# Softmax sums carried by DMA and mixed work spread over the attention steps in an eight-core encoder layer

## The reference, cut to what matters

```
a = rms_norm(h, g_mix);  z = a @ w_in            # 2048 -> q 1024, k 1024, v 1024, u 1024, gv 1024
q, k = partial_rope(q), partial_rope(k)          # first 16 of 64 dims
s_c  = softmax(q_c k_c^T / 8), c = 0, 1          # 8 heads, two components of 64 dims, 2048 keys
o    = rms_norm(s_0 v - lam * s_1 v) * 0.8       # per head, 128 wide
g    = gelu(u) * (w_spatial . layer_norm(gelu(gv)) + b)   # 128x128 position mixing in each chunk
h   += [o, g] @ w_out
h   += (silu(conv3(G)) * conv3(U)) @ w_down      # [G, U] = rms_norm(h) @ w_up, 2 x 5632
h   += (p @ w_ple_up) * sigmoid(rms_norm(h) @ w_ple_gate)
y    = rms_norm(h, g_final)
```

## Time and profile before

| | |
|---|---|
| time, median of 3 runs | 2069.48 us (2062.49 to 2089.54) |
| the profiled execution's own time | 2064.24 us |
| its span (slowest core, 7) | 2062.7 us |
| spans of the 8 cores | 2053.6 to 2062.7 us |
| granted TensorE clock, mean of each core | 0.983 to 0.987 of full speed |
| busy: TensorE, DVE, ACT, POOL | 1917.6, 999.0, 749.4, 186.3 us |

### The profile page before, as it was taken

The page is one execution under the profiler, slowest core; times in us unless marked ns, Lnnn a source line. Parts: engine busy times, 40 slices in busy tenths (PEclk is TensorE's granted clock), DMA queues, the critical chain, the costliest instruction groups (busy, mean ns, idle before and its releaser), DMA issues.

```text
span 2062.7 us, 31107 instructions; the slowest of 8 cores (2053.6 to 2062.7 us)
## 1 busy us (share of the span) xinstructions
PE 1917.6 (93%) x11708; PEld 1059.0 (51%) x11708; DVE 999.0 (48%) x1305; ACT 749.4 (36%) x1039; POOL 186.3 (9%) x281
## 2 busy tenths in 40 slices
PE   5988999987889999988999999999999999999994
PEld 1433455554445555545666654566654566644441
DVE  3645201254444544554566641366641366643667
ACT  4621111104887777765222210122210022233553
POOL 5600000000000000001000000000000010001000
PEclk9998999999999999999999999999999999999997
DMA  9750344366002333328644444444444464444603
GB/s 223 221 109 14 69 82 62 53 120 195 1 1 42 52 54 60 52 52 134 111 73 75 78 75 75 78 79 75 74 75 78 82 103 77 71 72 83 108 26 138
DMA packets 60371, 170.43 MB, mean 83 GB/s; under 512 B 10816, under 2 KB 15168, under 8 KB 60096
## 3 DMA queue, kind: packets, MB, share of 16 engines
q0 software_dynamic: 34992, 125.58, 36.3%
q1 hardware_dynamic: 25232, 42.86, 6.6%
HBM read 279.29 MB, written 8.39 MB: 139 GB/s over the span
## 4 chain that ended last, share of the span: by engine, by line
PE 81%; DVE 6%; ACT 5%; issue 4%; DMA 3%; SPq 1%; POOL 1%; DVEq 0%; ACTq 0%; POOLq 0%
PE ps L336 81%; ACT big L339 4%; DVE big L342 3%; DMA big<-xo 1%; SPq L559 1%; DVE big L354 1%; DVE big L345 1%; DMA big<-wup 1%; POOL big L349 1%; DVE big L351 1%; DMA big<-xa 0%; DVEq L170 0%; DMA big<-big 0%; DMA big<-posa 0%; DVE big L349 0%
## 5 line engine op out<-in xcount | busy, mean ns | idle before, releaser
L336 PE MATMUL ps<-big 128*128 128x342 bf16 (+3 forms) x11708 | 1917.6, 330 | 125.1 <-ACT big L339 51.0
L336 PEld LDWEIGHTS ps<-big 128*128 128x128 bf16 (+1 forms) x11708 | 1059.0, 98 | 982.1 <-issue 257.9
L339 ACT ACTIVATE big<-big 128x1024 f32<-128x1024 f32 (+8 forms) x547 | 423.4, 792 | 925.8 <-DVE big L342 703.0
L342 DVE TENSOR_TENSOR big<-big 128x342 f32<-128x342 f32 (+8 forms) x424 | 306.1, 735 | 224.0 <-ACT big L339 190.2
L339 ACT ACTIVATE big<-ps 128x684 bf16<-128x684 f32 (+1 forms) x432 | 294.6, 705 | 178.2 <-PE ps L336 173.0
L345 DVE SCALAR_TENSOR_TENSOR big<-big 128x1024 f32<-128x1024 f32 (+1 forms) x228 | 258.5, 1134 | 207.2 <-ACT big L339 197.6
L342 DVE TENSOR_TENSOR big<-ps,big 128x1026 f32<-128x1026 f32 (+4 forms) x239 | 210.7, 897 | 284.1 <-PE ps L336 271.0
L342 DVE TENSOR_TENSOR big<-big,ps 128x342 f32<-128x342 f32 (+1 forms) x96 | 83.1, 866 | 202.6 <-PE ps L336 201.4
L402 POOL DMA_DIRECT2D big<-wup x88 | 46.5, 528 | 539.4 <-PE ps L336 508.7
L339 ACT ACTIVATE big<-ps,big 128x512 bf16<-128x512 f32 x50 | 34.0, 686 | 159.4 <-PE ps L336 159.4
L402 POOL DMA_DIRECT2D big<-wo x48 | 25.5, 532 | 518.5 <-PE ps L336 508.9
(11 more groups left out here) (25 smaller groups left out, 64.5 us busy)
## 6 DMA issues: line engine op xcount, KB each, us to landing
big<-wup POOLq DMA_DIRECT2D x88, 512.0 KB, 5.7
big<-wo POOLq DMA_DIRECT2D x48, 512.0 KB, 5.1
big<-xa SPq DMA_DIRECT2D x32, 512.0 KB, 7.2
big<-wdn POOLq DMA_DIRECT2D x32, 480.0 KB, 5.3
big<-xo SPq DMA_DIRECT2D x16, 512.0 KB, 9.9
big<-wg POOLq DMA_DIRECT2D x16, 512.0 KB, 13.7
y<-big SPq DMA_DIRECT2D x32, 256.0 KB, 2.2
big<-wdn POOLq DMA_DIRECT2D x16, 448.0 KB, 4.9
```

Of the source, the lines that this page charges most:

```text
L336: P.op("pe", lambda e: e.matmul(out, lhsT=lhsT, rhs=rhs, start=start, stop=stop), reads=reads, writes=writes, inc=inc)
L339: P.op("act", lambda e: e.activation(out=out, in_=in_, func=func, **kw), reads=reads, writes=writes)
L342: P.op(en, lambda e: e.tensor_tensor(out=out, in0=a, in1=b, op=op), reads=reads, writes=writes)
```

## The change

- The first V half uses banks 6, 7, 0, 1, 2, 3 in turn. `halo_norm` is called between the two pairs of tables, not ahead of both.
- `spatial()` is taken out of the q stage. `spatial_mm` (bank 7 only) is called in steps 3, 8 and 12 of the units 0 to 5, the halo part after it.
- The loads of h move from the stage's end into steps 6 of the units 1 to 15, and to the attention's end.
- The sums are copied to `SM`, SP writes the 4 rows that differ to DRAM (into y, which is overwritten at the end), and two further DMAs read them back, spread over all 128 partitions, into `LA` and `LB`. DVE adds the two, ACT takes one `Ln` and one `Exp` of 684 columns. `sum3(selw[c])` and its `split3` are gone; `post_b` moves to step 1 of the unit after.
- The fill matmuls are spread over the steps 2 to 15 by `FILL`, two or three in each.
- At unit 23 seven more weight slots are opened where K lay. `hg`, `xp` and the FFN's buffers change places for that.
- At the attention's end the leftover fill and 15 of 16 matmuls of block 2's first tiles are issued ahead of the last unit's `post_b`; the copies for the FFN come out of `late`.
- At the final norm `Ln` is called once on a dummy, and the last squares go into the sum by a second matmul. Four multiplications of block 0 move behind it.

```diff
         def halo_norm():
-            rstd_bcast(ACC[0][:, 0:2], R_ACC[0], 2, rown[:, 1024:1026], R_rown[2], 4)
-            rstd_tok(ACC[0][:, 0:128], R_ACC[0], 1, 16, R_rtok[4], 5)
+            rstd_bcast(ACC[1][:, 0:2], R_ACC[1], 2, rown[:, 1024:1026], R_rown[2], 4)
+            rstd_tok(ACC[1][:, 0:128], R_ACC[1], 1, 16, R_rtok[4], 5)
         def pre_steps():
-            load_halo(0, 0)
+            load_halo(1, 0)
             yield
-            load_halo(0, 1)
+            load_halo(1, 1)
             yield
-            yield
+            P.inherit(R_tco, R_XS)
+            P.inherit(R_ang, R_XS + R_SQ + [R_ACC[0]])
+            yield from table_steps(0, 1024, TO, roth, R_roth, R_tco)
             halo_norm()
             yield
-            P.inherit(R_tco, R_XS)
-            P.inherit(R_ang, R_XS + R_SQ + R_ACC)
-            yield from table_steps(0, 1024, TO, roth, R_roth, R_tco)
             yield from table_steps(1, NT, (TC, TS), rown, R_rown, R_tca[0])
         steps = pre_steps()
@@ -749,7 +746,7 @@
         for hf_ in range(2):
             for t in range(8):
                 P.inherit(R_V[8 + t][hf_], [R_lam])
-        tok_proj(vitems, v_epi(0), [6, 7], hook)
+        tok_proj(vitems, v_epi(0), [6, 7, 0, 1, 2, 3], hook)
 ...
-        def spatial():
-            if sp_i[0] >= 16:
-                return
+        def spatial_mm():
             grp, hh = sp_i[0] // 8, sp_i[0] % 8
-            b = (6, 7)[sp_i[0] % 2]
-            sx, R_sx = SPT[sp_i[0] % 2], R_SPT[sp_i[0] % 2]
+            b = 7
+            sx, R_sx = SPT[sp_i[0] % 2], R_ut[sp_i[0] % 2]
 ...
-        SPT = [V(ZRO, F32, 512), V(ZRO + 2048, F32, 512)]
-        R_SPT = [Reg(), Reg()]
+        SPT = [ut[0][:, 0:512], ut[1][:, 0:512]]
 ...
-            else:
-                for _ in range(3):
-                    spatial()
-        while sp_i[0] < 16:
-            spatial()
 ...
+        def h_first(i, gate):
+            P.dma("sp", lambda e: e.dma_start(out=h[:, 2 * i:2 * i + 2, 0:512], in_=src_h[0][i]), DS_h[i], after=gate + oldh)
+            P.dma("sp", lambda e: e.dma_start(out=h[:, 2 * i:2 * i + 2, 512:684], in_=src_h[1][i][:, :, 0:172]), DS_h[i], after=oldh)
+            for j in (2 * i, 2 * i + 1):
+                for b in range(2):
+                    R_h[j][b].w = (DS_h[i].sem, DS_h[i].cnt)
+        def h_last(i, gate, after=()):
+            P.dma("sp", lambda e: e.dma_start(out=h[:, 2 * i:2 * i + 2, 684:1024], in_=src_h[1][i][:, :, 172:512]), DS_h[i],
+                  reads=[R_h[2 * i][0]], after=gate + list(after) + oldh)
+            for j in (2 * i, 2 * i + 1):
+                R_h[j][2].w = (DS_h[i].sem, DS_h[i].cnt)
+        def h_tail(after):
+            for i in range(2):
+                src = xh_d[i].rearrange("p (a b) -> p a b", a=8)[:, :, 0:2]
+                P.dma("sp", lambda e: e.dma_start(out=h[:, 8 * i:8 * i + 8, 1024:1026], in_=src), DS_hh, after=list(after) + oldh)
+            for j in range(16):
+                R_h[j][2].r = {0: (DS_hh.sem, DS_hh.cnt)}
+        SM = h[:, 0, 684:1026]
+        LB = [h[:, 1, 684:1026], h[:, 2, 684:1026]]
 ...
             if kt == 15:
                 cpy(XO, ps[:, 4:6, 0:NB], [Rb[4], Rb[5]], [R_XO])
-                split3(ps[:, 6, 0:NB], [Rb[6]])
+                cpy(SM, ps[:, 6, 0:NB], [Rb[6]], [R_sm])
+                yb = y_d[0, 4 * (k // 16 % 2):4 * (k // 16 % 2) + 4, 0:NB]
+                P.dma("sp", lambda e: e.dma_start(out=yb, in_=h[0:128:32, 0, 684:1026]), DS_yb, reads=[R_sm], writes=[R_yb])
+                P.dma("sp", lambda e: e.dma_start(out=LA, in_=yb[0:2, :].partition_broadcast(128)), DS_l, reads=[R_yb], writes=[R_la])
+                P.dma("sp", lambda e: e.dma_start(out=h[:, 1:3, 684:1026], in_=yb[2:4, :].partition_broadcast(128)), DS_l, reads=[R_yb],
+                      writes=[R_lb])
+                R_la.w = R_lb.w = (DS_l.sem, DS_l.cnt)
 ...
-        def post_a(u, c):
-            R, Rr = ((R0, R_r0), (R1, R_r1))[c]
-            sum3(selw[c])
-            act(R, ps[:, 7, 0:NB], AF.Ln, [Rb[7]], [Rr])
-            act(R, R, AF.Exp, [], [Rr], scale=-1.0)
-            if c == 0:
-                tt(OO, XO[:, 0, :], R, ALU.mult, [R_XO, Rr], [R_oo])
-            else:
-                stt(R, XO[:, 1, :], neglam, R, ALU.mult, ALU.mult, [R_XO, R_lam], [Rr])
-                tt(OO, OO, R, ALU.add, [Rr], [R_oo])
-                tt(RM, OO, OO, ALU.mult, [R_oo], [R_rm])
-                split3(RM, [R_rm])
+        def post_add(u):
+            for c in range(2):
+                tt(LA[:, c, :], LA[:, c, :], LB[c], ALU.add, [R_lb], [R_la])
+        def post_ln(u):
+            act(LA, LA, AF.Ln, [], [R_la])
+        def post_exp(u):
+            act(LA, LA, AF.Exp, [], [R_la], scale=-1.0)
+        def post_o(u):
+            tt(OO, XO[:, 0, :], LA[:, 0, :], ALU.mult, [R_XO, R_la], [R_oo])
+            stt(LA[:, 1, :], XO[:, 1, :], neglam, LA[:, 1, :], ALU.mult, ALU.mult, [R_XO, R_lam], [R_la])
+            tt(OO, OO, LA[:, 1, :], ALU.add, [R_la], [R_oo])
+            tt(RM, OO, OO, ALU.mult, [R_oo], [R_rm])
+            split3(RM, [R_rm])
         def post_b(u):
             sum3(onesb)
-            tsc(R0, ps[:, 7, 0:NB], 1.0 / 128, EPS, ALU.mult, ALU.add, [Rb[7]], [R_r0])
-        def post_c(u):
+            tsc(RM, ps[:, 7, 0:NB], 1.0 / 128, EPS, ALU.mult, ALU.add, [Rb[7]], [R_rm])
+        def post_rs(u, i):
+            if i == 0:
+                act(RM, RM, AF.Ln, [], [R_rm])
+            else:
+                act(RM, RM, AF.Exp, [], [R_rm], scale=-0.5)
+        def post_out(u):
             b, hh = units[u]
-            lnexp(R0, R_r0)
-            stt(mixA[:, hh, b * NB:(b + 1) * NB], OO, gsubc, R0, ALU.mult, ALU.mult, [R_oo, R_r0, R_lam], [R_qb[hh][b]])
+            stt(mixA[:, hh, b * NB:(b + 1) * NB], OO, gsubc, RM, ALU.mult, ALU.mult, [R_oo, R_rm, R_lam], [R_qb[hh][b]])
 ...
+        sp_done = [False]
+        wonce = []
         gen = itertools.chain(wout_gen(0, [7]), wout_gen(1, [7]))
+        FILL = [0, 0, 3, 2, 2, 2, 2, 2, 3, 2, 2, 2, 2, 3, 3, 2]
         nstep = 16 * 24
         for k in range(nstep + LAG):
+            u, st = k // 16, k % 16
+            if u == 23 and st == 0:
+                for i in range(7):
+                    sl = Slot(Z3 + i * 4096, True)
+                    P.inherit(sl.reg, R_kT[0][i] + R_kT[1][i])
+                    wfree.append(sl)
+                    wonce.append(sl.reg)
+                pump()
             if k < nstep:
                 emit_qk(k)
-            u, st = k // 16, k % 16
-            fl = 9 <= u < 24 and st in (1, 2, 3, 4, 9, 10, 11, 12)
-            if fl:
-                fill(gen, 2)
+            nf = FILL[st] if 9 <= u < 24 else 0
+            fill(gen, nf - nf // 2)
+            if u < 9 and st in (3, 8, 12):
+                if sp_i[0] < 16:
+                    spatial_mm()
+                elif not sp_done[0]:
+                    spatial_halo()
+                    sp_done[0] = True
+                    for r in R_hacc:
+                        P.inherit(r, R_ut)
             ka = k - LAG
+            if u >= 2 and st == 1:
+                post_b(u - 2)
             if ka >= 0 and ka % 16 != 0:
                 if ka % 16 == 1:
                     emit_av(ka - 1)
                 emit_av(ka)
-            if fl:
-                fill(gen, 2)
+            fill(gen, nf // 2)
+            if u >= 24:
+                continue
             if u < 23 and st == 9:
                 q_pad(u + 1)
-            if st in (7, 15):
-                flush_sq()
-            if u < 24:
-                if u >= 1 and st == 6:
-                    post_a(u - 1, 0)
-                if u >= 1 and st == 8:
-                    post_a(u - 1, 1)
-                if u >= 1 and st == 14:
-                    post_b(u - 1)
-                if u >= 2 and st == 0:
-                    post_c(u - 2)
-        post_c(22)
-        post_a(23, 0)
-        fill(gen, 16)
-        post_a(23, 1)
-        fill(gen, 16)
-        post_b(23)
-        post_c(23)
-        fill(gen, 1000)
-        flush_sq()
+            if st in (12, 14):
+                flush_sq(1)
+            gate = [R_P[k % NP]]
+            if st == 6:
+                if 1 <= u <= 4:
+                    h_first(u - 1, gate)
+                elif 7 <= u <= 8:
+                    h_first(2 * u - 10, gate)
+                    h_first(2 * u - 9, gate)
+                elif 10 <= u < 16:
+                    h_last(u - 8, gate)
+            if u >= 1:
+                if st == 8:
+                    post_add(u - 1)
+                if st == 10:
+                    post_ln(u - 1)
+                if st == 11:
+                    post_exp(u - 1)
+                if st == 11:
+                    post_o(u - 1)
+            if u >= 2:
+                if st == 3:
+                    post_rs(u - 2, 0)
+                if st == 4:
+                    post_rs(u - 2, 1)
+                if st == 5:
+                    post_out(u - 2)
 ...
```

(64 more changed lines are left out.)

84 lines of the change are left out of this document (38 added, 46 removed).

## The result

The changed kernel takes 2121.0 us (median of 4), the kernel before, on the same chip, 2066.1: ratio 1.024, 95% interval 1.016 to 1.032. It is slower; the forecast was 2011. The profiled execution has a span of 2117.1 us, against 2062.7. In some executions of every kernel the cores of one die ran at a lower clock (one of the changed kernel took 2434.67 us), and all ratios and intervals here leave those out. Tables and rows are of each kernel's slowest core, unless the text says that they are means of the eight.

What follows compares the result with a forecast made beforehand. TensorE, busy 1917.6 of 2062.7 us, was taken as the bound. Terms -4.5, -21.7, +8, -26, -7 and -1.7 sum to -53 from 2064.2: 2011 us, range 1990 to 2046 (main case's own range 1997 to 2027).

Steps and rivals of the forecast that it cites:

- V half: First V half: six banks only let TensorE run ahead, the `Sin`s still hold it; gain 4.5 us (2 to 20).
- q stage: Stage without spatial calls: q tiles run back to back, attention starts at 464.1, not 485.8; gain 21.7 us.
- The door: Attention's first steps: about 3.5 us ahead of attention, as before the change; no separate term in the sum.
- Units 0 to 8: Attention units without fill: the sums' new chain sets a floor of 17.0 us against 16.07 before; loss 8 us.
- R: Attention units: time of the sums' round trip through DRAM, taken as 6.6 us (4.4 to 13.4); unit floor R + 10.4.
- mildly late: Rival, attention units: R of 8.5 us makes the floor 18.9 us, total 2041 us; chance 0.17.
- Units 9 to 22: Attention units with fill (forecast for 9 to 23): 17.8 us each instead of 19.53; gain 26 us (12 to 30).
- Even fill: Units with fill: spreading the fill matmuls makes TensorE the slower engine in nearly every step, 17.8 us a unit.
- Unit 23 and the end: End of attention: gain 10 us, of which unit 23's crowded round trip gives back 3; net gain 7 us.
- Final norm: Final norm: table load goes behind ACT's wait, last addition ahead of the matmul goes; gain 1.7 us (1 to 2).
- The rival that ended slower: Attention units: round trip late enough to be slower; at R of 11.6 us the kernel passes 2111 us; chance 0.07.
- The prediction's own sign of failure: Attention units: prediction is wrong if XO copies lie over 19 us apart, with ACT or DVE waiting for a DMA.

Runs made afterwards that it cites:

- run 1: Changed kernel without the sums' round trip through DRAM (the additions read a constant, so sums are left out): 2064.5 us, ratio 0.9999.
- run 5: Changed kernel with two squares buffers, no early weight slots, no door wait, fill in blocks (steps 4 to 7, 10 to 13), tiles' squares later: 2078.7 us, ratio 1.0027.
- runs 1 to 4: run 1; changed kernel with second squares buffer (1.025); that without round trip, chain earlier (1.0231); two squares buffers, block fill, no early slots or door wait (1.0205).
- run 8: Changed kernel with the sums on TensorE again, no door wait: fill over 11 steps (ratio 1.0001), or in the earlier kernel's steps (0.9949).
- run 6: Changed kernel with the seven weight slots opened after the last `post_add` (2125.0 us, profiled), or left out, with two squares buffers and no door wait (ratio 1.0155).

## Why the prediction was wrong

The forecast was 53 us less, the profiled executions differ by 54 us more: a miss of 107 us. The units 9 to 22 make 46 of it, the units 1 to 8 20, unit 23 and the end of attention about 33.

**V half: right.** The banks let TensorE run ahead, the `Sin`s still held it: waits of 5.85 and 7.64 us, K's rotary part at 194.4 (forecast 194.5), 4.2 to 4.6 us won by the banks alone (forecast 4.5 for the part). The added table load took 1.28 us, and ACT worked again 0.01 us behind it (load at 178.24, `Sin` at 179.53).

**q stage: right, a little less than forecast.** From K's rotary part on to attention 17.4 us were won; the forecast had 18.7, and the stop of 1.59 us is about the difference. Up to attention it is 25.0 us in all (forecast 26.2), 22.0 in the mean of the eight cores. **The door** was missed: I let attention start on the q stage's end and did not ask what memory the first `Exp` writes. That cost 3.2 us.

**Units 0 to 8: mechanism right, R too small.** The floor of R + 10.4 holds: 7.5 gives 17.9 (18.1 measured), 8.8 in unit 8 gives 19.2 (19.7). In the units with spatial calls the unit is R + 11.2 (units 1 to 4). I took R = 6.6, from stores of y and a position load in the earlier trace rows; the mean is 8.7, and 2.1 us in eight units are 17 of the 20 us that this part was off. Without the trip these units take 16.64 us (run 1), 0.5 us more than before, so the spatial calls and all else cost about 4 of the 28 us. Of the rivals, the round trip "mildly late" named this.

**Units 9 to 22: the step that failed.** I worked out 17.8 us: TensorE's busy time of 17.2, 0.4 for one hand-over of bank 7, and small waits. The busy time was right, 17.06 us at full clock in run 5. What failed is the term for the waits, and that the clock would stay at its full level. The sum looked at one engine's load and not at the order in the other two engines' lists. It had 0.6 us of waiting, and the changed kernel waits 3.3 us a unit, and loses 0.7 us more at a granted clock of 0.96 (17.75 busy against 17.06).

DVE's block of eight instructions from `post_o` to the end of `split3` takes 4.6 us, and whatever stands behind it and feeds ACT or bank 7 stopped TensorE for 2.3 to 5.3 us (result, runs 1 to 4). The kernel before had seven of these eight in one block as well (815.80 to 819.81), with the addition into h behind them, but nothing on ACT asked for that addition until the `Square` 2.5 us later:

```profile
820.40 0.51 DVE L342 TENSOR_TENSOR big<-big,ps 128x342 f32<-128x342 f32 x1
...
823.43 0.48 ACT L339 ACTIVATE big<-big 128x342 f32<-128x342 f32 x1
```

So it was not the length of the block that was new, but what stood how close behind it. Measured were 21.1 us a unit, and 19.05 with the order mended (run 5): 2.0 of the 3.3 us by which this part was off. The rest is the floor and bank 7: R is 6.8 to 9.7 us in these units, and R + 11.0 gives 17.8 only at 6.8. Even fill was no gain either: 20.3 against 19.5 (run 8). No run came to 17.8, the best single units to 18.5.

**Unit 23 and the end: mis-sized.** I saw that seven weight loads share the DMA engines with the round trip, and gave them 3 us. It was 21.7 us of waiting in unit 23 and 8.7 in the last one. The row I had, 10.1 us for a wo load, was the landing of a weight in a queue with 12 of them, not of a small load behind seven. The sum also gave unit 23 the gain of 1.73 us of a full fill unit, though it took 17.9 and not 19.5 us before.

**Final norm: right** (1.4, forecast 1.7). Some 3 us in the FFN, which isn't changed, stay unexplained.

The rival that ended slower had the right place for half of the loss (the trip, some 50 us in run 1), but asked for R of 11.6 in every unit. What made the kernel slower was a smaller R and two further things that add to it. The prediction's own sign of failure, XO copies over 19 us apart with DVE or ACT waiting for a DMA, came in six of the eight units without fill; in the fill units the copies were 18.7 to 22.7 us apart, and in six of the 14 DVE waited for no DMA at all.

## What to carry to other kernels

When work is taken off the bounding engine, work out the new order on each of the other engines as well: a short call that feeds the bound is as late as the longest block ahead of it in its list, and as late as what it waits for in another engine's list. A transfer on which an in-order engine waits is priced with the traffic that will be beside it, and a burst of large loads is not put ahead of a small one that something waits for. And when a stage is made shorter, look up what memory the next one writes first.

## What the runs showed of the hardware

A round trip through DRAM (5.3 KB written and read back into 128 partitions, 342 KB twice) took 7.4 to 7.5 us from the copy's end to the first use in two units with no load of h and no fill, 1.7 of it from the write's issue to the reads'. With a load of h or fill beside it, it took 7.1 to 10.9, and 28 in unit 23. The second read and its landings in all units:

```profile
L1014 SPq DMA_DIRECT2D big<-y x24: 378/468/549, 484.2 to 978.0; - x24
...
DMA to landing us min/median/max: 4.5/5.7/21.9
```

The 21.9 is the one issued 11 us behind seven weight loads of 512 KB. The two loads of the last two columns of h, in pieces of 8 bytes, landed 3.4 and 3.8 us after issue in the changed kernel (at 991, when the burst was over), and 38.6 and 44.2 us after it when they were issued within 2 us of such a burst (run 6). And 8 cores doing the same is part of each of these numbers: no run here had fewer.
